# A 32-expert loop with the down product of one expert placed behind the next expert's gate and up products, in three split passes

## What is computed

```python
logits = xt @ router_w + router_b
top_vals, top_idx = lax.top_k(logits, 4)          # 4 of 32 experts
gates = softmax(top_vals)
gu   = xs @ w_gu[e] + b_gu[e]                     # 1024 -> 2048, columns interleaved
gate = minimum(gu[:, ::2], 7.0)
up   = clip(gu[:, 1::2], -7.0, 7.0)
act  = (up + 1.0) * (gate * sigmoid(1.702 * gate))
y    = act @ w_down[e] + b_down[e]                # 1024 -> 1024
out[tok] += y * gates
```

## Time and profile before

| | us |
|---|---|
| profiled span | 3126.7 |
| first gate and up bias product of tile 0 | 368.4 |
| first one of tile 1 | 422.7 |
| last down product done | 1688.1 |
| one turn of the loop, tiles 1 to 31 | 40.82 |
| TensorE busy over the span | 2762.4 (88%) |
| VectorE, ScalarE busy over the span | 1756.8 (56%), 1170.9 (37%) |

### The profile page before, as it was taken

How to read it: one execution, slowest core, us unless ns; L and a number is a source line. 1 busy time by engine, 2 the same in 40 slices (tenths; PEclk the granted TensorE clock), 3 DMA queues, 4 the chain that set the end, 5 groups by cost and what they waited for, 6 DMA issues and landing times.

```text
span 3126.7 us, 32895 instructions
## 1 busy us (share of the span) xinstructions
PE 2762.4 (88%) x11604; PEld 2039.8 (65%) x11604; DVE 1756.8 (56%) x1942; ACT 1170.9 (37%) x1248; POOL 279.3 (9%) x336
## 2 busy tenths in 40 slices
PE   6987589999999999999996673498999989799997
PEld 4766456666666666666664343476888868588885
DVE  5764646666555555666664973546763354443333
ACT  4232345555555555555552130233222232232321
POOL 1230310000000000000002900000110000000000
PEclk9998699999999999999998785798999999999998
DMA  6742579999999999999996109333774333223432
GB/s 238 251 112 102 178 283 334 335 341 335 336 334 330 333 331 330 335 332 337 335 338 220 40 0 100 46 100 116 221 211 109 92 94 81 67 81 94 112 93 64
DMA packets 368731, 634.93 MB, mean 203 GB/s; under 512 B 45020, under 2 KB 238756, under 8 KB 368484
## 3 DMA queue, kind: packets, MB, share of 16 engines
q1 hardware_dynamic: 346244, 539.29, 54.0%
q0 software_dynamic: 17296, 76.03, 7.2%
q10 hardware_dynamic: 5136, 18.88, 1.5%
HBM read 610.10 MB, written 24.58 MB: 203 GB/s over the span
## 4 chain that ended last, share of the span: by engine, by line
PE 79%; DVE 10%; DMA 4%; ACT 2%; SPq 2%; POOL 1%; issue 1%; DVEq 0%; POOLq 0%; ACTq 0%
PE bank L1933 22%; PE bank L1949 15%; PE bank L2094 10%; PE bank L2095 10%; PE bank L2100 10%; PE bank L1922 2%; SPq L480 2%; PE bank L1911 1%; PE bank L1917 1%; PE bank L1760 1%; DMA ring<-k_dram 1%; PE bank L1795 1%; DVE work L1497 1%; PE bank L1796 1%; PE bank L1797 1%
## 5 line engine op out<-in xcount | busy, mean ns | idle before, releaser
L1415 DVE TENSOR_TENSOR gu_lo<-ring,gu_hi_ca 128x2048 fp32r<-128x2048 f32 x128 | 290.7, 2292 | 461.4 <-ACT gu_hi_ca L870 461.2
L1949 PE MATMUL bank<-ring,work 128*128 128x512 f32 x1024 | 458.9, 601 | 22.0 <-ACT work L882 22.0
L1949 PEld LDWEIGHTS bank<-ring,work 128*128 128x128 f32 x1024 | 190.2, 191 | 257.3 <-issue 227.7
L1933 PE MATMUL bank<-gu_lo,xs_hi 128*128 128x512 f32 x1024 | 316.1, 390 | 0.0
L1415 DVE TENSOR_TENSOR gu_lo<-ring,gu_hi_nat 128x2048 fp32r<-128x2048 f32 x128 | 290.7, 2291 | 28.8 <-ACT gu_hi_nat L870 28.3
L2094 PE MATMUL bank<-h_hi,fin_hi 128*128 128x512 f32 x704 | 277.7, 395 | 22.1 <-ACT h_hi L972 22.1
L2095 PE MATMUL bank<-h_hi,fin_lo 128*128 128x512 f32 x704 | 276.4, 393 | 0.0
L870 ACT ACTIVATE gu_hi_nat<-ring 128x2048 fp32r<-128x2048 f32 x128 | 241.9, 1920 | 51.1 <-PE bank L1933 51.1
L870 ACT ACTIVATE gu_hi_ca<-ring 128x2048 fp32r<-128x2048 f32 x128 | 241.5, 1910 | 42.6 <-PE bank L1933 39.0
L1933 PEld LDWEIGHTS bank<-gu_lo,xs_hi 128*128 128x128 f32 x1024 | 192.5, 188 | 40.5
L1013 ACT ACTIVATE fin_hi<-rows 128x1024 fp32r<-128x1024 f32 x88 | 88.2, 1052 | 213.5 <-DMA rows<-in_w_ffn_in 213.5
(11 more groups left out here) (425 smaller groups left out, 4521.3 us busy)
## 6 DMA issues: line engine op xcount, KB each, us to landing
ring<-in_expert_w_gate_up SPq DMA_DIRECT2D x256, 1024.0 KB, 6.9
ring<-in_expert_w_down SPq DMA_DIRECT2D x128, 1024.0 KB, 5.8
rows<-in_w_ffn_in SPq DMA_DIRECT2D x88, 512.0 KB, 4.9
work<-in_w_ada POOLq DMA_DIRECT2D x64, 384.0 KB, 3.8
cb<-in_w_ada POOLq DMA_DIRECT2D x48, 384.0 KB, 4.7
y_dram<-cb ACTq DMA_DIRECT2D x32, 512.0 KB, 5.8
work<-in_w_ffn_out SPq DMA_DIRECT2D x8, 1408.0 KB, 7.7
rows<-in_w_ffn_out SPq DMA_DIRECT2D x8, 1408.0 KB, 6.9
```

The costliest lines, as they stand in the source:

```text
L1415: tt(gu_lo[:, q], slot[q], whole(gu_hi[q % 4]), ALU.subtract).then_inc(s_gu_lo, 1)
L1933: last = mm(ps[2 * h + n][:], x[:, k, :], w[:, 512 * n:512 * (n + 1)], start=False, stop=(k == KD - 1 and w is lo))
L1949: last = mm(ps[4 + n][:], act_t[h][:, k, :], slot[q][:, k % 2, 512 * n:512 * (n + 1)], start=False, stop=(h == 1 and k == 3))
```

## The change

- The down product of expert e−1 runs after the gate and up products of expert e. The first turn (expert 0) has no down product, and the last down product stands behind the loop.
- The down product is split as the others: ScalarE makes high parts of slots 8 to 11 too, VectorE low parts, and the transposed hidden rows get a high and a low part; 48 products instead of 16 plain f32 ones. Within a slot all products with the high weights come first and those with the low weights after them, each group behind its own semaphore.
- Both engines prepare slots three ahead of TensorE (`LEAD`), in four buffers `slot_hi`.
- SyncE's order follows: `load_up` of expert e+1, then `load_down` of expert e.
- The down bias leaves the loop. The gates are spread over the experts (VectorE), transposed (TensorE), copied (ScalarE); after `s_moe_done` TensorE multiplies them with all down biases in eight plain f32 products, and VectorE adds these to `rows` ahead of `combine`.
- The activation reads PSUM directly: sigmoid of the unclipped gate, capped by `SIG_MAX`, and three VectorE steps over 512 columns; the up bias is raised by 1 on GpSimd beforehand.
- The hidden rows are transposed into banks 6 and 7, which the tokens' transposes use too; PSUM is allocated in pairs of banks.
- SyncE's loads for the stage behind the experts (`p_rows`, `c_rows`, `ple_w_sb[0]`) wait for the last turn of the loop, no longer for the last gate and up products.

```diff
-        ps = [ctx.enter_context(nc.psum_tensor(f"bank{i}", [P, 512], F32)) for i in range(8)]
+        pairs = [ctx.enter_context(nc.psum_tensor(f"bank{i}", [P, 1024], F32)) for i in range(4)]
+        ps = [pairs[i // 2][:, 512 * (i % 2):512 * (i % 2 + 1)] for i in range(8)]
...
+            load_up(1, 1, 1)
+            with sp.Fori(1, E - 1) as e:
+                load_up(e + 1, e + 1, e * 12 - 3)
+                load_down(e, e, e * 12 + 5)
+            load_down(E - 1, E - 1, 12 * (E - 1) + 5)
...
+            pool.wait_ge(s_bias_in, 48)
+            up_bias = bias_rows.rearrange("e (f two) -> e f two", two=2)[:, :, 1]
+            pool.tensor_scalar(up_bias, up_bias, 1.0, None, ALU.add).then_inc(s_bias_one, 1)
...
+            def expert(e, stores, follows):
+
+                for j in range(12):
+                    high_ahead(e, j)
+                    if j == 1 and stores:
+                        store_y(e - 2, done_at(e - 1, 11) + 1, y_dram[bass.ds(e * P - 2 * P, P), :])
+                    if j == 4:
+                        hidden_high(e - 1, 0)
+                        hidden_high(e - 1, 1)
+                        sigmoid(e, 0, done_at(e, 3) + 1)
+                    if j == 8:
+                        tokens_columns(e + 1)
+                        sigmoid(e, 1, done_at(e, 7) + 1)
+                    if j == 9 and follows:
+                        pick_biases(e + 1)
...
+            step(tt(prod, hot, gates.unsqueeze(3).broadcast_to([P, NT, TOPK, E]), ALU.mult))
+            dve.tensor_reduce(logits, prod.rearrange("p i k e -> p i e k"), AXX, ALU.add).then_inc(s_prep_dve, 1)
...
+                dve.wait_ge(s_sig_ready, tile * 2 + (h + 1))
+                if not (isinstance(tile, int) and tile == 0):
+                    dve.wait_ge(s_actt_ps, tile * 2 + (h - 1))
+                v = pairs[h][:].rearrange("p (f two) -> p f two", two=2)
+                step(ts(act_n[h], v[:, :, 1], LIMIT + 1.0, 1.0 - LIMIT, ALU.min, ALU.max))
+                step(stt(act_n[h], t_s[h], SIG_MAX, act_n[h], ALU.min, ALU.mult))
+                stt(act_n[h], v[:, :, 0], LIMIT, act_n[h], ALU.min, ALU.mult).then_inc(s_act_ready, 1)
...
+            def expert(e):
+
+                for j in range(12):
+                    low_ahead(e, j)
+                    if j == 1:
+                        swiglu(e - 1, 1)
+                    if j == 5:
+                        hidden_low(e - 1)
+                    if j == 7:
+                        swiglu(e, 0)
+                    if j == 9:
+                        tokens_low(e + 1)
...
+            for i in range(NT):
+                dve.wait_ge(s_gates_ps, i + 2)
+                tt(rows[:, i, :], rows[:, i, :], pairs[i][:], ALU.add).then_inc(s_prep_dve, 1)
...
+            def matmuls(banks, lhs, hi, lo, begins, ends, ready):
+
+                for lower in range(2):
+                    if lower:
+                        pe.wait_ge(s_slot_lo, ready)
+                    else:
+                        pe.wait_ge(s_slot_hi, ready)
+                    for k in range(2):
+                        for x in ((lhs[0],) if lower else lhs):
+                            for n in range(2):
+                                last = mm(ps[banks + n], x[:, k, :], (lo if lower else hi)[:, k, 512 * n:512 * (n + 1)],
+                                          start=(begins and lower == 0 and k == 0 and x is lhs[0]),
+                                          stop=(ends and lower == 1 and k == 1))
+                last.then_inc(s_slot_done, 1)
...
+            def expert(e):
+
+                pe.wait_ge(s_pick, e + 1)
+                pe.wait_ge(s_xst_ready, e * 2 + 2)
+                pe.wait_ge(s_act_ready, e * 2 - 1)
+                biases(0)
+                for j in range(4):
+                    up(j, hi_of(e, j), split_at(e, j) + 1)
+                hidden_columns(e - 1)
+                biases(1)
+                for j in range(4, 8):
+                    up(j, hi_of(e, j), split_at(e, j) + 1)
+                hidden_taken(e - 1)
+                tokens_columns(e + 1)
+                pe.wait_ge(s_y_sb, e * 2 - 1)
+                for j in range(8, 12):
+                    down(j - 8, hi_of(e, j), split_at(e, j) + 1)
```

More of the change, by code:

```diff
@@ L528, in load_slot, with load_up, load_down @@
                 load(slot[q], src.rearrange("p e k n -> p (e k) n"), s_slot_in[q])
[L530 to L538, removed]
+            def load_up(tile, expert, used):
+                for q in range(8):
+                    sp.wait_ge(s_slot_done, used + q)
                     load_slot(q, expert)
+            def load_down(tile, expert, used):
+                for d in range(4):
+                    sp.wait_ge(s_slot_done, used + d)
+                    load_slot(8 + d, expert)
             sp.wait_ge(s_wout_ready, 2 * NT)
@@ L872, in pick_biases, with high_ahead @@
+            def high_ahead(e, j):
+                if is_split(e, j) and is_split(*ahead_of(e, j)):
+                    split_high(*ahead_of(e, j))
             def pick_biases(index):
                 act.activation(pick[:], pick_e[0:2 * E, bass.ds(index, 1)].broadcast_to([2 * E, P]), ACT.Copy).then_inc(s_pick, 1)
[L875 to L901, removed]
@@ new lines, in _ @@
+            tokens_columns(1)
+            sigmoid(0, 1, 8)
+            pick_biases(1)
+            expert(1, False, True)
+            with act.Fori(2, E - 1) as e:
+                expert(e, True, True)
+            expert(E - 1, True, False)
+            for j in range(SPLIT_DOWN):
+                high_ahead(E, j)
+            store_y(E - 2, done_at(E - 1, 11) + 1, y_dram[P * (E - 2):P * (E - 1), :])
+            for h in range(2):
+                hidden_high(E - 1, h)
+            store_y(E - 1, done_at(E, 3) + 1, y_dram[P * (E - 1):, :])
@@ L1417, in tokens_low, with hidden_low @@
+            def hidden_low(tile):
+                for h in range(2):
+                    dve.wait_ge(s_actt_hi, tile * 2 + (h + 1))
+                    tt(act_lo[h], ps[6 + h].rearrange("p (k t) -> p k t", k=4), whole(act_hi[h]),
+                       ALU.subtract).then_inc(s_actt_lo, 1)
             def tokens_low(tile):
@@ L1971, in _ @@
+            tokens_columns(1)
+            with pe.Fori(1, E) as e:
+                expert(e)
+            pe.wait_ge(s_xst_ready, 2 * E + 2)
+            hidden_columns(E - 1)
+            hidden_taken(E - 1)
+            pe.wait_ge(s_y_sb, 2 * E - 1)
+            for j in range(4):
+                down(j, hi_of(E, j), split_at(E, j) + 1)
             extra = pe.value_load(smi[0:1, 72:73], min_val=0, max_val=MAX_EXTRA)
```

328 lines of the change are left out of this document (182 added, 146 removed).

## The result

| | before | changed |
|---|---|---|
| median of the timed executions, us | 3121.36 (3120.61 to 3123.78) | 2996.8 (2994.5 to 2999.53) |
| profiled span, us | 3126.7 | 2994.3 |
| one turn of the loop, us | 40.82 | 36.18 |
| last down product done, us | 1688.1 | 1558.5 |

What follows compares the result with a forecast made beforehand. TensorE was taken to bound the expert loop's turn. Terms of −127.1 us for the loop, +1.1 ahead and +1.7 behind summed to −124.3, taking 3121.55 to 2997 us, range 2984 to 3040.

Steps and rivals of the forecast that it cites:

- What bounds the turn: Expert loop: TensorE bounds the turn before and after, which falls from 40.8 to 36.4 us; chance 0.62.
- Down product: TensorE's loop turn: 14.19 us of plain f32 products become 48 fp32r products of 11.10, saving 3.09 us.
- Cover of VectorE: Loop turn: VectorE's 33.5 us fit into 36.4, about 2 us spare; rival that VectorE sets the turn, 3022 us, 0.20.
- ScalarE: Loop turn: 22.06 us plus four casts at 1.92 make 29.7 us, which fits into 36.4.
- DMA: Loop loads: 13.63 MB a turn fit in 32.5 to 34.2 us; rival that DMA sets the turn, 3047 us, 0.12.
- Start of the loop: Tile 1's first product at 405.2 us, after TensorE idled, with 2.9 us added for the low clock.
- Drain: Behind the last turn: 10.5 us up to the products, then 48 products; 24.5 us, between 21 and 27.
- last cast 1.9 after the last slot: First step of the pipeline's end: ScalarE's last cast is done 1.9 us after the last weight slot.
- the prediction's own sign (ends over 27 us): Sign that the forecast is wrong: the pipeline's ends cost more than 27 us.
- Ahead of the loop: Bias chain before the loop: shorter ScalarE and VectorE steps, but a GpSimd step ahead of them; net +1.1 us.
- Behind the loop: Bias product of 11 us, then one VectorE add of 1.28: +1.7 us, between 0 and +5.
- Slower through `hidden_taken`: Rival in the loop: TensorE's wait for the hidden rows' low part grows until the clock falls; 3211 us, chance 0.03.

Runs made afterwards that it cites:

- the one with all edits: Changed kernel with tile 1's gather early, last expert's down product plain, half the later gate weights loaded behind the gathers, bias product not awaiting stored outputs: 2970.39 us.

## Why the prediction was right, point by point

- **What bounds the turn: right, and shown.** 36.18 us for the 36.4 of the forecast. The first two stretches of 48 measured the 11.1 taken, the down stretch 10.89: 0.22 us a turn, 6.8 us in 31. The down stretch stands behind token transposes and the other two behind a bias pair, which is where I look for the 0.22; no run shows it.
- **Down product: nearly the right saving, wrongly assigned.** 3.09 were put down to the split; 14.19 against 10.89 is 3.30. The 14.19 was two interrupted passes; in one piece the plain pass is 13.73. So the split is worth 2.87, and some 0.4 belong to the joining of the passes, which I had not told apart. The bias (0.71 for 0.66) holds, and what is left agrees with the wait of 0.7.
- **Cover of VectorE: right in size and place.** 33.0 us for 33.5. The hidden rows' low parts were ready 2.7 us ahead of the token transposes that overwrite their banks (2.0 forecast), the next tile's 2.4 ahead of their bias pair (2.2). The run with one VectorE step more confirms 2 us of room by sum.
- **ScalarE: 27.1 for 29.7.** I had carried over the turn of before whole, with its two table loads of 1.28 us; the new loop shows none. It made no difference, since even 29.7 would have left 6 us of room.
- **DMA: right.** 377 GB/s without a wait, and a level of 411, between the 398 and 420 that the rows showed. The share of 1.00 is no sign of a limit.
- **Start of the loop: 406.2 for 405.2,** the slow clock 3.2 us (1121.6 us for 31 turns of 36.18, 1124.8 measured) for 2.9.
- **Drain: 27.5 us, forecast 24.5, between 21 and 27. The step that failed** is "last cast 1.9 after the last slot". It took the weights as loaded. The last four down slots can only be loaded when TensorE leaves the previous expert's, so the first is issued at 1522.82 and casts end only at about 1538, 7 us behind the turn's end for the 1.9 taken. Up to the products that makes 14.2 us for 10.5, with TensorE idle for 12.5 of them and not 8; the products then took 13.3 for 14.0. The plain product, which needs no cast, shortens the drain by 10.8 us. By the prediction's own sign (ends over 27 us) this term was wrong, though the total was not.
- **Ahead of the loop: +1.1 forecast, nothing to be seen.** GpSimd's step took 2.88 us (3.0 taken), but the biases are off the chain: it runs through the routing. Tile 0 starts 3.1 us earlier in this pair of profiles, within the 8.6 us over which that start varies.
- **Behind the loop: +3.6 for +1.7.** The bias product took 13.26 us for the 11 assumed, at a granted clock of 0.53:
```profile
1562.40:1576.90 14.50, 13.26 (x16) 4.79 (x16) 4.82 (x5) 0.00 (x0) 10.87 (x12) 0.53 0.85 299
```
  and the additions then stand ahead of `combine`. It was inside the 0 to 5 given.
- **The sum.** Against the forecast's terms: start +1.0, ahead of it −1.1, clock +0.3, turns −6.8, drain +3.0, behind +1.9: −1.7, so 126.0 us saved up to the `combine` step for 124.3. The profiled spans differ by 132.4; the other 6 us appear in the last stage, whose code is the same, and are within its spread. The medians differ by 124.6. The mechanism was right, but that the forecast comes within 0.3 us is luck: errors of 2 to 7 us cancel in it, and the spread of the executions alone is larger.
- **Slower through `hidden_taken`: nothing of it.** TensorE doesn't wait there.

## What to carry to other kernels

When a change makes the bounding engine faster, write down the busy sum of every other engine over the new turn, then measure the room with a dummy step or a dummy load: here two dummy runs each enclosed the point at which VectorE (above 35.1 us of work a turn, by 37.4) and the loads (above 405 GB/s, by 411) take over. A pipeline pays at its ends: ask of each of its last steps not only how long it takes but when its operands can be loaded at all, and let the last round use the form with the shortest chain even if it is the slower one on TensorE. An epilogue transfer issued early can stand ahead of the one short store that everyone waits for.

## What the runs showed of the hardware

- The loads of one core alone ran at 405 GB/s with no wait of TensorE and levelled off at 411; the busy share read 1.00 at 377, 1.02 at 405 and 1.03 at 411, so the share doesn't tell how much is left.
- A plain f32 product of 128 by 512 columns holds the chain for 13.73 / 16 = 0.86 us, an fp32r one for 10.89 / 48 = 0.227: three split products cost 0.68 for 0.86.
- GpSimd's three short steps a turn got longer when the order against VectorE shifted, their own work being unchanged: 18.8 us busy in ten turns of the changed kernel, 25.1 and 36.5 with one and two VectorE steps more. It isn't VectorE's load as such. With the two extra loads and no extra VectorE step it was 34.6 us in 27 steps, and the whole rise is in one address step on 128x1 numbers, which ran beside a 128x2048 low part (0.19 us in the changed kernel):
```profile
L711 POOL TENSOR_TENSOR smi<-smi 128x1 int32<-128x1 int32 x9 | 19.2, 2129 | 0.7
```
  In the prologue a step of 128x64 took 0.33 us or 2.26. The Trainium skill names a cause ("SBUF — State Buffer", Who interferes with whom: a VectorE instruction with two SBUF inputs contends with a GpSimd instruction that reads SBUF). Which of the two pays differs: in the loop the low parts kept their 2.29 us, in the earlier trace rows it was VectorE's step that took 2.83 us for 1.22. No run here took VectorE away from it.
- With 4.3 to 11 us of TensorE idle time ahead of them, 48 products took 13.2 to 14.0 us for 11.1; the shortest idle time (4.3 us, in the run with the early gather and in the one with all edits) still cost 2.1. Behind the copies between loop and plain drain (2.7 us of idle time) the granted clock stayed at 1.00.
